# Routing in two parts, the new tokens second in the output projection, and a weight load in halves

## The chip, the cores and the metric

The kernel runs on one core of a Trainium2 chip, in one launch. The metric is the device time in microseconds (us); lower is better. Times of a stage are read from one profiled execution, in us from the start of its span.

## The reference, cut to what matters

One decoder layer: 512 prompt tokens and 64 new tokens (8 sequences of 8), width 1024, all in 32-bit floats. Two token mixers are merged into `m`; the tail, which the change touches, is:

```
x = x + g1 * (m @ w_o)                                  # w_o 1024 x 1024
h = rmsnorm(x, norm2) * (1 + sc2) + sh2
glog = h @ w_rg + b_rg ; elog = h @ w_re + b_re         # 4 groups, 32 experts
group = top-1 of glog ; experts = top-2 of elog inside the group
weight = softmax(two logits) * softmax(glog)[group]
for each expert e: out += weight_e * ((silu(h @ w_gate_e) * (h @ w_up_e)) @ w_down_e)   # 1024->256->1024
x = x + g2 * out ; y = rmsnorm(x, final_norm)
```

Each token goes to two of 32 experts. The weights of all experts are read from HBM: gate and up are 1 MB each, down is 1 MB, so 3 MB an expert.

## The kernel before, in words

The tail is one block of five instruction streams (sync SP, gpsimd POOL, scalar ACT, tensor PE, vector DVE) built from three stages, one behind the other on every engine: `merge_programs` (merge of the mixers, `w_o`, second norm, router logits), `expert_programs` (routing and experts) and `final_programs`. The order on each engine is written out by hand, and semaphores tie the engines together; an engine that waits holds everything behind it.

**`w_o` and logits.** The 576 tokens are five tiles (`NT = 5`; tile 4 has the 64 new tokens). `o_tile(t)` (L2140 to L2152) makes two 512-column products for a tile, and tile 4 makes both at once in two halves of the array (L2143). For each half DVE multiplies by the gate (L2277) and adds the residual (L2280); ACT squares (L2085), POOL makes the reciprocal root (L2044, L2046), DVE makes the normed rows (L2286, L2288). SP stores `x2` (L2013) and ACT stores `h2` (L2090) to scratch in HBM. PE transposes `h2` (L2161), ACT copies it out (L2094), PE makes 36 logits (L2172), DVE adds the bias (L2265). Tiles go 0, 1, 2, 3, 4. The per-sequence shift, scale and gate of the new tokens (`mod_new`) come by 16 DMAs from ACT's queue (L2076, L2077); DVE first waits for them when it reaches tile 4 (L2271).

**Routing.** When all five tiles' logits are there, DVE chooses group and experts for all tiles in one pass (L2567 to L2587), PE counts tokens per expert by bf16 products with 0/1 matrices, DVE works out for each of the 10 token-choice columns a block, a step and a slot (L2594 to L2630), PE multiplies one-hot matrices into a table of 25 steps (L2493), and DVE writes `pairs` and `toks` (L2640 to L2646). POOL waits for that table, then gathers rows of `h2` by indirect DMA (L2423).

**Experts.** Each of 17 fixed steps does two experts, 64 rows each. In a step PE does 8 transposes (L2502), 32 gate/up matmuls (L2514), 2 small transposes (L2521) and 16 down matmuls (L2531). Ahead of step 0 PE does 20 matmuls for the last block's rows (L2540). Gate/up weights (4 MB a step) have three buffers, down weights (2 MB a step) four. SP issues the loads (L2704, L2713) in this order: step 0, down 0, gate/up 1, the five `x2` stores, down 1 behind the last `w_o` product, down 2 behind the last `x2` store, gate/up 2 behind the `h2` stores, down 3 behind `overd` (the end of the routing's use of memory that down buffer 3 covers), then gate/up 3 behind `gmm >= 1`, that is the last gate/up matmul of step 0, and from there gate/up s+3 behind step s's gate/up product, down s+4 behind step s's down product.

The core of SP's loop, before:

```
sp.wait_ge(overd, 1)
load_down(sp, m, ins, 3, (6, 7))
...
if max(lo, GU_BUFS) <= g < hi:
    sp.wait_ge(gmm, s + 1)
    load_gate_up(sp, m, ins, g, experts(g))
```

Of the kernel before, what the change touches and what calls it, by code (L numbers as in the profile page):

```python
# [9 lines left out]
U32 = mybir.dt.uint32  # L10
# [1890 lines left out]
ROUTE_CONST = 64  # L1901
ROUND = 12582912.0
# [25 lines left out]
def expert_memory(nc, m):  # L1928
# [14 lines left out]
    m.iota, m.rc, m.rcb = tail("iota", [128, 128]), tail("route_const", [128, ROUTE_CONST]), tail("route_const_bf", [128, 280], BF16)  # L1943
    m.x2 = Region(nc, base + 99520)("x2", [128, NT, D])


def merge_programs(nc, m, ins, st, psum, sem):
# [16 lines left out]
    ss, rstd = sb(96256, "x2_ss", [128, NT]), sb(96288, "x2_rstd", [128, NT])  # L1964
# [34 lines left out]
    def sync(sp):  # L1999
# [11 lines left out]
        for t in range(NT):  # L2011
            sp.wait_ge(x2d, 2 * t + 2)
            sp.dma_start(m.x2_dram[tile_cols(t), :], m.x2[0:ROWS[t], t, :]).then_inc(x2st, 16)  # L2013
            if t == NT - 2:
                sp.wait_ge(omm, 10)
                load_down(sp, m, ins, 1, (2, 3))
        sp.wait_ge(h2d, NT)
        sp.wait_ge(x2st, 16 * NT)
        load_down(sp, m, ins, 2, (4, 5))
        sp.wait_ge(h2tr, NT)  # L2020
# [4 lines left out]
    def gpsimd(pool):  # L2025
# [14 lines left out]
        pool.dma_start(m.rbias[:, NG:36], ins["b_re"][0].partition_broadcast(128)).then_inc(rld, 16)  # L2040
        for t in range(NT):
# [3 lines left out]
            pool.wait_ge(rsd, 2 * t + 1)  # L2045
            p.tensor_tensor(q, q, m.half[:, 0:1], ALU.pow).then_inc(rsd, 1)  # L2046

    def scalar(act):
# [30 lines left out]
        act.wait_ge(init, 2)  # L2079

        def square(t):
            act.wait_ge(x2d, 2 * t + 2)
            if t:
                act.wait_ge(xsq, t)
            a.activation(junk[0:ROWS[t], :], m.x2[0:ROWS[t], t, :], ACT.Square, accum_out=ss[0:ROWS[t], t:t + 1]).then_inc(xsq, 1)  # L2085

        def keep_h2T(t):
            r = ROWS[t]
            act.wait_ge(h2d, t + 1)
            act.dma_start(m.h2_dram[tile_cols(t), :], h2[0:r, t % 2, :]).then_inc(h2st[t % 2], 16)  # L2090
            act.wait_ge(h2tr, t + 1)
            if t:
                act.wait_ge(lmm, t)
            a.copy(h2T[:, :, 0:r].rearrange("p (a c) t -> p a c t", a=2),  # L2094
                   psum[:, 4:6, :].rearrange("p a (c t) -> p a c t", t=128)[:, :, :, 0:r]).then_inc(h2ev, 1)
        square(0)
        for t in range(1, NT):
            keep_h2T(t - 1)
            square(t)
        keep_h2T(NT - 1)  # L2100

    def tensor(pe):
# [35 lines left out]
        def o_tile(t):  # L2138
            if t == 4:
                pe.wait_ge(oev, 6)  # L2140
                for c in range(KC):
                    for j in range(2):
                        last = te.matmul(psum[64 * j:64 * j + 64, j, :], mT[:, c, tile_cols(t)], wo[j][:, c, :],  # L2143
                                         start=c == 0, stop=c == KC - 1, tile_position=(0, 64 * j))
                last.then_inc(omm, 2)
                return
            for j in range(2):
                i = 2 * t + j
                if i >= 4:
                    pe.wait_ge(oev, i - 3)  # L2150
                for c in range(KC):
                    last = te.matmul(psum[0:ROWS[t], i % 4, :], mT[:, c, tile_cols(t)], wo[j][:, c, :], start=c == 0, stop=c == KC - 1)  # L2152
                last.then_inc(omm, 1)

        def h2_transposes(t):
            r = ROWS[t]
            pe.wait_ge(h2d, t + 1)
            if t:
                pe.wait_ge(h2ev, t)
            for c in range(KC):  # L2160
                last = te.transpose(psum[:, 4 + c // 4, 128 * (c % 4):128 * (c % 4) + r],  # L2161
                                    h2[0:r, t % 2, 128 * c:128 * c + 128], m.ident[0:r, 0:r])
            last.then_inc(h2tr, 1)

        def logits(t):
            r = ROWS[t]
            pe.wait_ge(h2ev, t + 1)
            pe.wait_ge(rld, 64)
            if t >= 2:
                pe.wait_ge(ld, t - 1)  # L2170
            for c in range(KC):
                last = te.matmul(psum[0:r, 6 + t % 2, 0:36], h2T[:, c, 0:r], wr[:, c, :], start=c == 0, stop=c == KC - 1)  # L2172
            last.then_inc(lmm, 1)

        o_tile(0)
        for t in range(1, NT):
            o_tile(t)
            h2_transposes(t - 1)
            logits(t - 1)
        h2_transposes(NT - 1)  # L2180
        logits(NT - 1)

    def vector(dve):
# [78 lines left out]
        def add_logits(t):  # L2262
            r = ROWS[t]
            dve.wait_ge(lmm, t + 1)
            v.tensor_tensor(m.logits[0:r, t, :], psum[0:r, 6 + t % 2, 0:36], m.rbias[0:r, :], ALU.add).then_inc(ld, 1)  # L2265

        for t in range(NT):
            r = ROWS[t]
            if t == NT - 1:
                dve.wait_ge(nld, 32 * NB)  # L2270
                v.scalar_tensor_tensor(modn[0:64, 2, :], modn[0:64, 2, :], 1.0, n2[0:64, :], ALU.add, ALU.mult).then_inc(sc2, 1)  # L2271
                dve.wait_ge(sc2, 2)
            for j in range(2):
                i = 2 * t + j
                dve.wait_ge(omm, i + 1)
                rows = slice(0, r) if t < 4 else slice(64 * j, 64 * j + 64)
                v.tensor_tensor(xs[0:r, j, :], psum[rows, i % 4, :], mod(t)[rows, 0, GW * j:GW * j + GW], ALU.mult).then_inc(oev, 1)  # L2277
                dve.wait_ge(oev, i + 1)
                x = m.x2[0:r, t, GW * j:GW * j + GW]
                v.tensor_tensor(x, x, xs[0:r, j, :], ALU.add).then_inc(x2d, 1)  # L2280
            dve.wait_ge(rsd, 2 * t + 2)
            if t >= 2:
                dve.wait_ge(h2tr, t - 1)
                dve.wait_ge(h2st[t % 2], 16 * (t // 2))
            h = h2[0:r, t % 2, :]
            v.scalar_tensor_tensor(h, m.x2[0:r, t, :], rstd[0:r, t:t + 1], mod(t)[0:r, 2, :], ALU.mult, ALU.mult).then_inc(hsc, 1)  # L2286
            dve.wait_ge(hsc, t + 1)
            v.tensor_tensor(h, h, mod(t)[0:r, 1, :], ALU.add).then_inc(h2d, 1)  # L2288
            if t:
                add_logits(t - 1)  # L2290
        add_logits(NT - 1)
# [4 lines left out]
def route_constants(nc, m, step):  # L2296
# [11 lines left out]
    step(p.iota(ints[:, 0:10], pattern=[[1, 2], [0, NT]], base=0, channel_multiplier=2))  # L2308
    step(p.tensor_copy(m.rcb[:, 256:266], ints[:, 0:10]))
    step(p.iota(ints[:, 0:10], pattern=[[0, 2], [1, NT]], base=1, channel_multiplier=0))  # L2310
# [3 lines left out]
def expert_programs(nc, m, ins, psum, sem):  # L2314
# [93 lines left out]
    def gpsimd(pool):  # L2408
# [24 lines left out]
        def run(lo, hi):  # L2433
# [8 lines left out]
            for s in range(lo, hi):  # L2442
                if s + 2 < hi:
                    gather(s + 2)
# [509 lines left out]
```

## Time and profile before

| | us |
|---|---|
| time, median of 3 runs (lowest, highest) | 1181.98 (1181.97, 1183.64) |
| the profiled execution's own time | 1181.74 |
| its span | 1180.0 |
| PE busy | 1069.7 (91%) |
| DVE busy | 560.2 (47%) |
| ACT busy | 250.2 (21%) |
| POOL busy | 154.4 (13%) |

The profiled execution spends 1.7 us outside its span. Busy shares are means over the whole layer; the change sits in the stretch from 784 us on, and the rows below are taken there. "PEclk" is TensorE's granted clock as a share of full speed. A DMA's "landing" is counted from its issue.

### The profile page before, as it was taken

The numbers are of one execution on the slowest core, as the hardware profiler recorded it, in microseconds if no ns is written. First come the engines' busy times: TensorE is split into PE (matmuls) and PEld (weight loads), VectorE is DVE, ScalarE is ACT, GpSimd is POOL, SyncE is SP. The second block draws the span as 40 slices with busy tenths as digits, with TensorE's granted clock in tenths as the row PEclk, the third lists the DMA queues.
The fourth block names the chain that finished last, engine by engine and source line by source line (L and its number), as shares of the span: only waits on it lengthen the run. The fifth ranks groups of instructions, "written<-read, shape, count | busy, mean of one in ns | idle before, by whom it ended". The sixth has DMA issues, their size and how long they took to land. (4 is left out here: it accounts for less than half of the span.)

```text
span 1180.0 us, 15016 instructions
## 1 busy us (share of the span) xinstructions
PE 1069.7 (91%) x5862; PEld 703.7 (60%) x5862; DVE 560.2 (47%) x1109; ACT 250.2 (21%) x673; POOL 154.4 (13%) x299
## 2 busy tenths in 40 slices
PE   5999998999999999899999999999946998978786
PEld 3455777777777887887577777754423333322222
DVE  3123737467788494475754455443264111110126
ACT  3100010567622222464111010101110110100011
POOL 3000500012314000041100000100011211111101
PEclk8999998999999999899999999999967999998998
DMA  9995543252414443124462422359176999999975
GB/s 334 340 258 181 192 77 75 43 128 69 74 50 72 107 80 73 37 73 144 125 223 83 111 75 89 123 138 327 77 286 222 416 420 415 418 419 418 412 290 175
DMA packets 96852, 226.32 MB, mean 192 GB/s; under 512 B 21422, under 2 KB 40167, under 8 KB 84082
## 3 DMA queue, kind: packets, MB, share of 16 engines
q1 hardware_dynamic: 86998, 202.70, 52.5%
q10 hardware_dynamic: 4660, 12.75, 3.1%
q0 software_dynamic: 5120, 9.88, 2.3%
q8 instruction: 48, 0.79, 0.3%
q14 instruction: 26, 0.21, 0.1%
HBM read 210.60 MB, written 23.08 MB: 198 GB/s over the span
## 5 line engine op out<-in xcount | busy, mean ns | idle before, releaser
L2514 PE MATMUL ps<-w_gate_up,xT 128*64 128x512 f32 x528 | 129.5, 630 | 20.5 <-DMA w_gate_up<-w_e_up 20.5
L2514 PEld LDWEIGHTS ps<-w_gate_up,xT 128*64 128x64 f32 x528 | 41.2, 145 | 105.9 <-issue 76.8
L2676 DVE TENSOR_TENSOR act<-silu_gate,ps 128x256 f32<-128x256 f32 x17 | 7.1, 420 | 199.1 <-ACT silu_gate L2469 199.1
L695 PE MATMUL ps<-hT,w_ring 128*128 128x288 f32 x384 | 97.5, 414 | 3.7 <-PEq L105 3.7
L695 PEld LDWEIGHTS ps<-hT,w_ring 128*128 128x128 f32 x384 | 73.9, 195 | 23.9 <-issue 4.0
L2531 PE MATMUL ps<-w_down,actT 128*64 128x512 f32 x264 | 62.1, 599 | 8.8 <-DVE actT L2680 8.8
L1345 PE MATMUL ps<-hT,w_ring 128*128 128x288 f32 x264 | 67.8, 407 | 0.0
L1630 DVE SCALAR_TENSOR_TENSOR conv_y<-z_staged,convT,conv_y 128x600 f32<-128x600 f32 x72 | 59.7, 842 | 9.3 <-ACT conv_y L1080 7.5
L1345 PEld LDWEIGHTS ps<-hT,w_ring 128*128 128x128 f32 x264 | 49.4, 190 | 13.1 <-issue 0.5
L2531 PEld LDWEIGHTS ps<-w_down,actT 128*64 128x64 f32 x264 | 18.0, 136 | 41.2 <-issue 29.1
L2429 POOL DMA_INDIRECT pair_scratch<-y_block,pairs x16 | 16.0, 1003 | 200.7 <-ACT y_block L2477 200.7
L2469 ACT ACTIVATE silu_gate<-ps 128x256 f32<-128x256 f32 x17 | 6.5, 383 | 129.7 <-PE ps L2514 129.7
L2477 ACT COPY y_block<-ps 128x1024 f32<-128x1024 f32 x16 | 16.2, 1012 | 83.7 <-PE ps L2531 83.7
L2152 PE MATMUL ps<-w_ring,mT 128*128 128x512 f32 x64 | 31.8, 654 | 2.3 <-issue 2.3
L2113 PE MATMUL ps<-T_mixers,w_ring 128*128 128x288 f32 x128 | 33.7, 406 | 0.0
L1080 ACT ACTIVATE conv_y<-z_staged,convT 128x600 f32<-128x600 f32 x24 | 19.1, 796 | 67.7 <-DVE z_staged L1710 58.9
L1411 PE MATMUL ps<-hT,w_ring 128*128 128x288 f32 x128 | 32.8, 411 | 0.0
L423 PE MATMUL ps<-w_ring,hT 128*128 128x512 f32 x64 | 31.1, 643 | 1.2 <-DVE hT L572 1.2
L2210 DVE TENSOR_TENSOR pair_sums<-pair_sums,ps 128x288 f32<-128x288 f32 x14 | 6.4, 454 | 50.7 <-PE ps L2113 50.7
L1411 PEld LDWEIGHTS ps<-hT,w_ring 128*128 128x128 f32 x128 | 23.8, 190 | 10.5 <-issue 3.0
L454 PE MATMUL ps<-w_ring,hT 128*128 128x512 f32 x64 | 29.7, 625 | 0.0
L2502 PEld LDWEIGHTS ps<-ident,x_gathered 128*128 128x128 f32 x136 | 17.1, 196 | 19.3 <-issue 13.0
(539 smaller groups left out, 1995.2 us busy)
## 6 DMA issues: line engine op xcount, KB each, us to landing
w_down<-w_e_down SPq DMA_DIRECT2D x32, 1024.0 KB, 23.6
w_ring<-w_in SPq DMA_DIRECT2D x15, 2048.0 KB, 13.8
w_gate_up<-w_e_gate SPq DMA_DIRECT2D x30, 1024.0 KB
w_gate_up<-w_e_up SPq DMA_DIRECT2D x30, 1024.0 KB
w_ada_slots<-w_ada SPq DMA_DIRECT2D x8, 2048.0 KB, 8.4
w_ada_slots<-w_ada SPq DMA_DIRECT2D x4, 1024.0 KB, 15.0
w_ring<-w_pa SPq DMA_DIRECT2D x2, 2048.0 KB, 7.9
w_ring<-w_pb SPq DMA_DIRECT2D x2, 2048.0 KB, 7.9
```

The costliest lines, as they stand in the source:

```text
L423: last = te.matmul(psum[:, zv_bank(t), :], m.hT[:, c, tile_cols(t)], zv0[:, c, :], start=c == 0, stop=c == KC - 1)
L454: last = te.matmul(psum[:, zv_bank(i), :], m.hT[:, c, tile_cols(t)], zv1[:, c, :], start=c == 0, stop=c == KC - 1)
L695: last = nc.tensor.matmul(psum[:, bank + hf, 0:HALF], w[:, c, 128 * q:128 * q + 128], x[:, c, HALF * hf:HALF * hf + HALF], start=c == 0, s ...
L1080: a.activation(y[:, n % 2, 0:TAPPED], stage(n)[:, 0:TAPPED], ACT.Copy, scale=m.convT[:, CH[n]:CH[n] + 1]).then_inc(tap, 1)
L1345: last = te.matmul(psum[:, k % 4, 0:HALF], w[:, c, :], x(c), start=c == 0, stop=c == 3)
L1411: last = te.matmul(psum[:, b, 0:HALF], w0[:, c, 128 * n:128 * n + 128], hT[:, c, HALF * hf:HALF * hf + HALF], start=c == 0, stop=c == KC - 1)
L1630: v.scalar_tensor_tensor(out, stage(n)[:, j:j + TAPPED], wt, out, ALU.mult, ALU.add).then_inc(cstep if j < HIST else conv, 1)
L2113: last = te.matmul(psum[:, n % 8, 0:HALF], w[:, c, :], x[:, c, :], start=c == 0, stop=c == 3)
L2152: last = te.matmul(psum[0:ROWS[t], i % 4, :], mT[:, c, tile_cols(t)], wo[j][:, c, :], start=c == 0, stop=c == KC - 1)
L2502: last = te.transpose(psum[:, 2 + c // 4, 128 * (c % 4):128 * (c % 4) + 128], xg[:, s % 2, c::KC], m.ident[:, :])
L2514: last = te.matmul(psum[side(u), s % 2, :], xT[:, s % 2, c, side(u)], gu[s % GU_BUFS][:, u, :, c, :], start=c == 0, stop=c == KC - 1)
L2531: last = te.matmul(psum[side(u), 4 + hf, :], aT[:, s % 2, c, side(u)], wd[s % WD_BUFS][:, u, c, 512 * hf:512 * hf + 512], start=c == 0, st ...
```

## The change

**`merge_programs`.** The tiles are taken in the order `ORDER = (0, 4, 1, 2, 3)`; a position p stands for the place in that order. PE's order is:

```
+        o_half(0, 0, whole)
+        o_half(0, 1, whole)
+        o_new(1)
+        h2_transposes(0)
+        o_half(2, 0, range(0, 2))
+        logits(0)
+        o_half(2, 0, range(2, KC))
+        for p in range(2, NT):
+            if p > 2:
+                o_half(p, 0, whole)
+            h2_transposes(p - 1)
+            if p == 3:
+                constant_logits()
+            o_half(p, 1, range(0, 4))
+            logits(p - 1)
+            o_half(p, 1, range(4, KC))
+        early_counts()
+        last_transposes(0)
+        logits(END, range(0, 4))
+        table(0, EARLY_POS)
+        last_transposes(1)
+        logits(END, range(4, KC))
+        late_counts()
+        table(EARLY_POS, NT)
```

The last tile's rows are transposed and multiplied with the router before their norm: `scaled(j)` is x2 times the scale, and the reciprocal root and the part of the logits that comes of the shift (`constant_logits`) are put in when the logits are read. DVE's order from the second tile on:

```
+        second_norm(0)
+        dve.wait_ge(nld, 32 * NB)
+        v.scalar_tensor_tensor(modn[0:64, 2, :], modn[0:64, 2, :], 1.0, n2[0:64, :], ALU.add, ALU.mult).then_inc(sc2, 1)
+        dve.wait_ge(sc2, 2)
+        residual(1, 0)
+        residual(1, 1)
...
+        choose_experts(nc, dve, m, r, 0, EARLY_POS, 0)
+        second_norm(3)
+        choose_experts(nc, dve, m, r, 0, EARLY_POS, 1)
+        residual(END, 0)
+        scaled(0)
+        split_pairs(nc, dve, m, r, 0, EARLY_POS)
+        add_logits(3)
+        slot_rows_of(nc, dve, m, r, 0, EARLY_POS, psum[:, 2, 0:96])
+        residual(END, 1)
+        scaled(1)
+        dve.wait_ge(rsd, 2 * END + 4)
+        dve.wait_ge(x4tr, 2)
+        v.scalar_tensor_tensor(h, h, rstd[:, END:], modp[:, 1, :], ALU.mult, ALU.add).then_inc(h2d, 1)
+        v.scalar_tensor_tensor(m.logits[:, END, :], psum[:, 6 + END % 2, 0:36], rstd[:, END:], r.const[:, :], ALU.mult, ALU.add).then_inc(ld, 1)
+        choose_experts(nc, dve, m, r, EARLY_POS, NT, 0)
+        choose_experts(nc, dve, m, r, EARLY_POS, NT, 1)
+        split_pairs(nc, dve, m, r, EARLY_POS, NT)
+        slot_rows_of(nc, dve, m, r, EARLY_POS, NT, psum[:, 3, 0:64])
+        ... 3 small operations, then the table: pairs and toks of the 16 regular steps
```

`choose_experts` is the choice of L2570 to L2587 for the positions lo to hi (12 operations in part 0, 6 in part 1, one more at its end). `split_pairs` makes the step one-hots by 6 small operations. `slot_rows_of` waits for PE's counts, then does 2 products, 2 sums and 2 * (hi - lo) comparisons against the slot numbers. The slot of a choice comes straight from the count, and the old chain over blocks and overflow steps (12 small operations with their own one-hots) is put off:

```
+        def run(lo, hi):
+            if lo == 0:
+                over_blocks()
+                weights()
             x_evacuate(lo)
+            if lo == 0:
+                over_counts()
+                over_pairs()
             for s in range(lo, hi):
+                if s == 1:
+                    over_slots()
                 dve.wait_ge(sgd, s + 1)
+                if s == 1:
+                    over_table_columns()
...
                 if s + 1 < hi:
                     x_evacuate(s + 1)
```

`over_slots()` is 12 small operations, 3 on 90 elements and 10 comparisons on 128 elements, and ends in

```
+            last.then_inc(over_hot, 1)
+            dve.wait_ge(over_hot, 1)
+            v.nop().then_inc(constd, 1)
```

PE makes the table of the overflow steps by 20 small matmuls behind step 1's gate/up product.

**SP.** Down 2 waits for the last `x2` store as before, gate/up 2 for the `h2` stores. Then:

```
-        sp.wait_ge(overd, 1)
-        load_down(sp, m, ins, 3, (6, 7))
+        load_down_of(sp, m, ins, 3, 0, 6)
+        sp.wait_ge(constd, 1)
+        load_down_of(sp, m, ins, 3, 1, 7)
...
-                if max(lo, GU_BUFS) <= g < hi:
+                if g == GU_BUFS:
+                    sp.wait_ge(first_half_used, 1)
+                    load_gate_up_half(sp, m, ins, g, experts(g), 0)
+                    sp.wait_ge(gmm, s + 1)
+                    load_gate_up_half(sp, m, ins, g, experts(g), 1)
+                elif max(lo, GU_BUFS) <= g < hi:
                     sp.wait_ge(gmm, s + 1)
                     load_gate_up(sp, m, ins, g, experts(g))
```

`load_down_of` loads one expert's 1 MB; `load_gate_up_half` loads 4 times 512 KB. `first_half_used` is raised behind the 16th of step 0's 32 gate/up matmuls. The upper half of down buffer 3 lies over the constants that routing and `over_slots` read.

**POOL.** The waits of the routing go, but for those on the `h2` stores and the table; the clearing of the gathered rows goes, and that of `y_last` (L2416) moves behind the first two gathers. `final_programs` reads the weights by position; nothing else of it changes.

## Rows read from the trace of the kernel before

**Rows 1.** Stretches: PE, PEld, DVE, ACT, POOL busy; PEclk, DMA share, GB/s.
```profile
836.00:838.00 2.00, 2.00 (x4) 0.85 (x3) 1.52 (x3) 0.00 (x0) 0.00 (x0) 0.50 0.00 0
875.00:887.00 12.00, 0.83 (x7) 0.61 (x7) 10.92 (x44) 0.32 (x2) 0.89 (x1) 0.50 1.01 426
887.00:893.00 6.00, 0.93 (x10) 0.64 (x10) 5.56 (x26) 0.00 (x0) 1.23 (x2) 0.50 0.08 34
904.00:910.00 6.00, 5.96 (x32) 2.57 (x28) 0.42 (x2) 0.38 (x1) 0.00 (x0) 1.00 0.22 40
911.00:1117.00 206.00, 178.52 (x804) 67.58 (x800) 28.22 (x43) 20.55 (x29) 29.25 (x29) 0.96 1.02 418
```
**Rows 2.** Timeline of SP's issues from 835 us: start, us, what.
```profile
864.42 0.47 SPq L2013 DMA_DIRECT2D x_scratch<-x  x1
870.65 1.04 SPq L2713 DMA_DIRECT2D w_down<-w_e_down  x2
...
892.64 0.81 SPq L2713 DMA_DIRECT2D w_down<-w_e_down  x2
908.56 0.33 SPq L2704 DMA_DIRECT2D w_gate_up<-w_e_gate  x1
```
**Rows 3.** The chain that ended last, from 891 us: start, us, what.
```profile
891.00 0.19 DVE toks L2646
891.47 4.58 DMA x_gathered<-h_scratch,toks
...
901.50 7.02 PE ps L2514 x32
```
**Rows 4.** Timeline of PE, from 780 us.
```profile
792.48 7.03 PE L2152 MATMUL ps<-w_o_second,mT 128*128 128x512 f32 x16
834.78 8.81 PE L2152 MATMUL ps<-w_ring,mT 128*128 128x512 f32 x16
...
852.43 1.97 PE L2172 MATMUL ps<-w_router,h2T 128*128 128x36 f32 x16 [1.10 <-ACT h2T L2094]
854.34 0.64 PE L2143 MATMUL ps<-w_ring,mT 128*64 128x512 f32 x1
...
861.36 1.09 PE L2161 MATMUL ps<-ident,h 128*128 128x128 f32 x8
```
**Rows 5.** ACT's DMA queue from 781.6 to 810 us: packets, MB, share of 16 engines.
```profile
q10 hardware_dynamic: 256, 1.05, 14.2%
```
**Rows 6.** Timeline of DVE, from 835 us.
```profile
850.50 0.69 DVE L2277 TENSOR_TENSOR x_step<-ps,mod_prompt 128x512 f32<-128x512 f32 x1 [5.45 <-PE ps L2152]
855.69 1.23 DVE L2288 TENSOR_TENSOR h<-h,mod_prompt 128x1024 f32<-128x1024 f32 x1
856.93 1.21 DVE L2271 SCALAR_TENSOR_TENSOR mod_new<-mod_new,norm2b 64x1024 f32<-64x1024 f32 x1
874.12 0.89 DVE L2578 TENSOR_SCALAR pen<-gone 128x20 f32<-128x20 f32 x1
875.75 0.33 DVE L2567 TENSOR_TENSOR one<-em,mv 128x160 f32<-128x160 f32 x1
885.54 0.17 DVE L2624 SCALAR_TENSOR_TENSOR slot<-side__5605,s 128x10 f32<-128x10 f32 x1
886.86 2.04 DVE L2630 TENSOR_SCALAR onehot_slot<-iota,slot 128x128 bf16<-128x128 f32 x10
910.34 1.21 DVE L2668 COPY xT<-ps 128x1024 f32<-128x1024 f32 x1
```
**Rows 7.** POOL's clearing beside the choice, from its timeline.
```profile
873.17 1.80 POOL L2415 MEMSET x_gathered<- 128x2048 f32 x1 [6.70 <-DVE logits L2265]
```
**Rows 8.** Gathers, issue to landing: the one of 891.47, of 892.95, all 17.
```profile
x_gathered<-h_scratch,toks POOLq DMA_INDIRECT x1, 4.6
x_gathered<-h_scratch,toks POOLq DMA_INDIRECT x1, 9.5
x_gathered<-h_scratch,toks POOLq DMA_INDIRECT x17, 10.3
```

More of the change, by code:

```diff
@@ L1901 @@
 ROUTE_CONST = 64
+ORDER = (0, 4, 1, 2, 3)
+POS = {t: p for p, t in enumerate(ORDER)}
+PROWS = [ROWS[t] for t in ORDER]
+EARLY_POS = 3
+EMPTY = 2304.0
+SIDE = 1024.0
 ROUND = 12582912.0
@@ new lines, in split_pairs @@
+def split_pairs(nc, dve, m, r, lo, hi):
+    v = nc.vector
+    at, shape = slice(lo, hi), [128, 2, hi - lo, NE // 2]
+    one = r.one[:, :, at, :].rearrange("p k t (s u) -> p k t s u", u=2)
+    for k in range(2):
+        last = v.tensor_tensor(r.onehot_step[:, k, at, :], one[:, k, :, :, 0], one[:, k, :, :, 1], ALU.add)
+    last.then_inc(r.split, 1)
+    dve.wait_ge(r.split, 1 if lo == 0 else 2)
+    for x, part in enumerate((r.high, r.low)):
+        for k in range(2):
+            last = v.tensor_tensor(r.parts[:, x, k, at, :], r.onehot_step[:, k, at, :],
+                                   part[:, k, at].unsqueeze(2).broadcast_to([128, hi - lo, NE // 2]), ALU.mult)
@@ new lines, in slot_rows_of, with step @@
+def slot_rows_of(nc, dve, m, r, lo, hi, counts):
+    v = nc.vector
+    at, n = slice(lo, hi), hi - lo
+    def step(i):
+        r.n += 1
+        i.then_inc(r.step, 1)
+        dve.wait_ge(r.step, r.n)
+    dve.wait_ge(r.counted, 1 if lo == 0 else 2)
+    for k in range(2):
+        i = v.tensor_tensor(r.prod[:, k, at, :], r.one[:, k, at, :], counts.rearrange("p (t e) -> p t e", e=NE), ALU.mult)
+        if k:
+            step(i)
+    for k in range(2):
+        i = v.tensor_reduce(r.v[:, k, at], r.prod[:, k, at, :], AX.X, ALU.add)
+        if k:
+            step(i)
+    for k in range(2):
+        for p in range(lo, hi):
+            last = v.tensor_scalar(r.onehot_slot[:, k, p, :], m.slots[:, :], r.v[:, k, p:p + 1], None, ALU.is_equal)
+    last.then_inc(r.hot, 1)
@@ L2096, in scalar, with square @@
-        square(0)
[L2097 to L2100, printed above, removed]
+        act.wait_ge(init, 3)
+        act.wait_ge(mld, 32)
+        act.wait_ge(win, 7 * PAIRS)
+        a.copy(h2[64:65, 1, :], modp[64:65, 1, :]).then_inc(shd, 1)
+        def square(p):
+            rows = PROWS[p]
+            act.wait_ge(x2d, 2 * p + 2)
+            if p:
+                act.wait_ge(xsq, p)
+            a.activation(junk[0:rows, :], m.x2[0:rows, ORDER[p], :], ACT.Square, accum_out=ss[0:rows, p:p + 1]).then_inc(xsq, 1)
@@ L2175, in tensor, with o_half @@
[L2175 to L2181, printed above, removed]
+        def o_half(p, j, cs):
+            tile, i = ORDER[p], 2 * p + j
+            if i >= 4 and cs[0] == 0:
+                pe.wait_ge(oev, i - 3)
+            for c in cs:
+                last = te.matmul(psum[:, i % 4, :], mT[:, c, tile_cols(tile)], wo[j][:, c, :], start=c == 0, stop=c == KC - 1)
+            if cs[-1] == KC - 1:
+                last.then_inc(omm, 1)
@@ new lines, in late_counts, with table @@
+        def late_counts():
+            pe.wait_ge(r.chosen, 2)
+            te.matmul(psum[:, 3, 0:32], r.strict, both[:, 3, :], start=False, stop=False)
+            te.matmul(cut(psum[:, 3, 32:96]), r.onesb, two(both[:, 3, :]), start=False, stop=False)
+            te.matmul(psum[:, 3, 32:64], r.strict, both[:, 4, :], start=False, stop=False)
+            te.matmul(psum[:, 3, 64:96], r.onesb, both[:, 4, :], start=False, stop=True).then_inc(r.counted, 1)
+        def table(lo, hi):
+            pe.wait_ge(r.hot, 1 if lo == 0 else 2)
+            for p in range(lo, hi):
+                rows = PROWS[p]
+                for k in range(2):
+                    for x in range(2):
+                        last = te.matmul(psum[:, 2, 128:144], r.onehot_slot[0:rows, k, p, :], r.parts[0:rows, x, k, p, :],
+                                         start=p == k == x == 0, stop=p == END and k == x == 1)
+            if hi == NT:
+                last.then_inc(r.tabled, 1)
@@ L2260, in vector @@
         dve.wait_ge(init, 2)
[L2262 to L2290, printed above, removed]
```

550 lines of the change are left out of this document (345 added, 205 removed).

## The prediction

> **What bounds the kernel now.** The view by stretches comes first, since the page's busy shares average over stages with other limits. From 911 to 1117 us the DMA engines are full (share 1.02, 418 GB/s) while PE works 178.5 of 206 us [rows 1]. 418 GB/s times 206 us is 86 MB: the weights from gate/up 3 on, and the gathers and scatters beside them. The expert stage is therefore a train of bytes of fixed length, and its end moves with its start. Just before it, from 904 to 910, the DMA engines do nearly nothing (40 GB/s) [rows 1]. What starts the train is the next question, and SP's issues answer it: gate/up 3 is issued at 908.56 [rows 2], 0.04 us after the first gate/up product ends at 901.50 + 7.02 = 908.52 [rows 3]. The chain back from there: table written at 891.20, gather landed at 896.05, transposes and 20 extra matmuls to 901.50 [rows 3]. So the quantity to follow is the instant at which gate/up 3 gets the DMA engines. The weights ahead of it are hidden whatever their order, if they have landed by then: from 887 to 893 the queues ran dry too (34 GB/s) [rows 1].
>
> **A, the `w_o` stage: to the end of its last product.** Before, it ends at 861.36, where tile 3's transposes start [rows 4]. A half tile of `w_o` is 6.86 us (the row reads 7.03, of which 0.17 lies over the next one's start), tile 4's double product 861.36 - 854.34 = 7.02, eight transposes 1.09, a tile's logits 854.34 - 852.43 = 1.9, and each time PE idled 1.10 for ACT's copy [rows 4]. The new order fills those three 1.1 us holes with `w_o` columns (-3.3), but now has all four sets of transposes and logits ahead of the last product, instead of three (+2.9), and the constant product (+0.2).
> Then two stalls. First, the new tokens come second, and their scale and gate come by 16 DMAs that now are needed early. By 810 us ACT's queue had moved 1.05 MB, just what those 16 DMAs write (8 x 96 KB + 8 x 32 KB) [rows 5]; I take them as landed at 810. DVE is ready for them at 805.7 (tile 0's second half ends at 792.48 + 6.86 = 799.34, and the norm comes 6.4 later: from 850.50, 0.2 after such an end, to 855.69 + 1.23 = 856.92 with gate, add, square, root and two norm operations, less 0.2 for a logits addition between [rows 4, 6]). Then 1.21 for the scale [rows 6], four half operations of 0.73, 2.1 for square and root, 2.5 for the norm: transposes of the new tokens from about 818.8, while PE has nothing left from 816.1. Stall 2.7. Second, the norm of position 3 stands behind 12 operations of the early choice; it is ready about 0.3 us after PE. Last, the clock: in the stretch behind 834.78 a half tile took 8.81 instead of 6.86 with a granted clock of 0.50, that is 1.2 of 2.4 GHz [rows 1, 4], after PE had paused for ACT's copy and worked on small tiles. It is inside the 861.36. I keep it, since the new order has a pause too.
> 861.36 - 3.3 + 2.9 + 0.2 + 2.7 + 0.3 = 864.1. Term A: +2.7. Ends: -1.9 (transfers by 806, no dip), +4.5 (transfers at 812).
>
> **B, from the last product to the table.** Before: 861.36 to 891.20, 29.8 us. After, from T = the last product's end: counts 0.7; DVE's early slots (2 products and 2 sums of some 0.25 each, 6 comparisons of 0.2 [rows 6]) to T+2.8; residual and scale to T+5.0; square, four small POOL operations to T+6.4; one 1.28 us operation on 1024 columns and the logits to T+7.9. Late choice: 12 + 7 dependent operations at about 0.2 on 20 elements and 0.26 on 64 (0.17 and 0.33 are the rows for 10 and 160, and a gap of 0.03 follows [rows 6]) = 4.6, to T+12.5. `pen` took 0.89 before on 20 elements [rows 6], and it ended at 875.01 with POOL's clearing, 873.17 + 1.80 = 874.97 [rows 7]; that clearing is gone, so I take 0.2. Six small operations 0.9, late slots 1.6, three small operations 0.3, the last 8 table products 0.7, two table operations 0.4: T+16.3. Term B: 16.3 - 29.8 = -13.5. What went: the pass over all five tiles becomes one over two, and the 12-step chain over blocks goes behind the first gather. Ends: -15 to -11 (cold PE, `pen` at 0.9). The table then stands at 864.1 + 16.3 = 880.4.
>
> **C, the gather.** Before, issued at 891.47 and landed 4.58 later [rows 3]: nothing was on the queues (34 GB/s from 887 to 893 [rows 1]), and down 3 was issued only at 892.64 [rows 2]. After, issued at about 880.7, where down 2 and gate/up 2 are in flight. The last `x2` store, now 512 KB, goes at about T+4.3 and lands near 875 (before: issue 864.42, down 2 behind its landing at 870.65 [rows 2]); down 2 follows, `h2`'s last store at T+7.9 lets gate/up 2 go by 877, and with down 3's first MB behind that the DMA engines have 7.3 MB, some 17 us at 426 GB/s [rows 1], to about 893. A gather among loads takes 9.5 (the one of 892.95) or 10.3 (median of 17, nearly all in the full stretch) [rows 8]. I take 10.0 as against 4.6. Term C: +5.4. Ends: 0 and +6.7.
> The Trainium skill (DMA: Bandwidth & Descriptors, section Queues, rings and completion order) says that each DMA engine takes turns between its queues, a packet at a time. By that alone the gather would lose only its turn, the first rival below, and the sum would come to +0.3; the trace's gathers among loads do not agree (9.5, 10.3).
> Gathered: about 890.9. DVE's four small operations over counts and the 10 weight columns (about 5.5 us) end before that and cost nothing. If the gather came at 885 they would come to the edge of the path.
>
> **D, from the gather to step 0's last gate/up matmul.** Transposes, 20 matmuls, 32 matmuls: 908.52 - 896.05 = 12.5 [rows 3], unchanged. It ends at 903.4. Term D: 0.
>
> **E, from there to gate/up 3.** Before 0.04. After, the text of SP decides. SP takes its instructions in order, and ahead of both halves of gate/up 3 stands the wait for `constd` and the second MB of down 3. `constd` is raised at the end of `over_slots`, and DVE runs that under `s == 1`: behind step 0's activation and behind `x_evacuate(1)`. Before, DVE left that copy at 910.34 + 1.21 = 911.55 [rows 6], 3.0 us after 908.52. Then 12 dependent operations at 0.17 with gaps, 2.5; three on 90 elements, 0.6; 10 comparisons 2.0 [rows 6]; the last wait 0.1: 5.2. So `constd` comes 8.2 us after the product whose middle was to release the first half: both halves' own waits have long been met, and the halving wins nothing. Queued behind that wait on SP: down 3's second half, gate/up 3, down 4 and all the rest; for 13 us or so, from 893 to after 911, the DMA engines stand idle again.
> Behind `constd` comes 1.05 MB of down 3, which used to be landed by then: 1.05 / 0.418 = 2.5 us [rows 1]. In return step 0's scatter and the fourth gather fall partly into the idle time: about half of 1 MB, 1.0 us. Term E: 8.2 + 0.1 + 2.5 - 1.0 = +9.8. Ends: +8.3 and +11.5.
> Halves of 512 KB with 4 KB rows: no row prices this alone; zero, at most 0.3.
>
> **Sum.** A +2.7, B -13.5, C +5.4, D 0, E +9.8: +4.4. On the profiled execution's 1181.74 that is 1186.1; the median of the runs shown, 1181.98, is 0.2 above it. I forecast 1186.0. Behind the train nothing is changed: last step and final stage keep their length.
>
> **Rivals.**
> Gather hardly slowed (18%). Its 128 rows are 0.52 MB, 1.25 us at 418 GB/s; at half that rate it takes 1.25 us more than the 4.6 alone, 5.9. For it: it has a queue of its own, and the loads fill only SP's. Against: both rows of gathers among loads. At 4.6 to 5.9 us: 1180.7 to 1182.0, no slower than before. It decides from a gather below about 8 us (then the sum is under +2.4).
> The train is not what counts (8%): PE's steps set the end, and starting step 0 earlier pays at once: -5.1 (908.5 to 903.4), 1176.6. It needs PE to be the later one at step 3 and on. For it: PE's share is high. Against: 178.5 of 206 us busy beside a DMA share of 1.02 [rows 1]. This one ends faster than before; it decides if the idle DMA time up to 911 can be caught up by less than 11 us of slack.
> More is late than I count (12%): `over_slots` slowed by PE's and POOL's traffic, or the late choice on a cold PE, or the new tokens' transfers at 812: +3, 1189.
> My forecast (62%), by itself 1182.5 to 1189.
> That the change doesn't do what it says is part of the forecast: the halves are not loaded while the first product runs.
>
> **Range and chances.** The ends of the terms and the rivals give 1178.5 to 1190.5 for 8 in 10. 0.2% is 2.4 us, about what a measurement of this kernel tells from none. Faster than 1179.6: nearly all of the second rival, a third of the first: 14%. Within: most of the rest of the first and a quarter of the forecast's case: 27%. Slower: 59%.
>
> **What would show it.** SP waits for DVE's `constd` and issues down 3's second half about 8 us after step 0's last gate/up matmul; DMA share near 0 for over 10 us before; table some 11 us earlier than 891.2; first gather 9 to 10 us; PE idle 2 to 3 us ahead of the new tokens' transposes. Wrong, if gate/up 3 is issued before step 0's product ends, or if the first gather lands in 5 us, or if PE does not wait for weights from step 4 on.

## The result and the profile after

Timed beside each other, eight runs of each kernel: before 1182.1 us (1178.1 to 1184.9), after 1188.9 us (1185.7 to 1192.2). The ratio is 1.0059, with a 95% interval of 1.0043 to 1.0074: slower by 7.0 us (6.8 between the medians). The forecast was 1186.0, slower by 4.4. The profiled executions have spans of 1180.0 and 1187.0, so they carry the same 7.0.

First SP, from its timeline of the changed kernel (start, us, what it issued):

```profile
874.49 0.96 SPq L2987 DMA_DIRECT2D w_down<-w_e_down  x2
...
877.41 0.65 SPq L2973 DMA_DIRECT2D w_gate_up<-w_e_up  x1
878.10 32.83 SPq L2978 DMA_DIRECT2D w_down<-w_e_down  x2
910.97 0.80 SPq L2954 DMA_DIRECT2D w_gate_up<-w_e_gate  x1
```

The last row but one holds two DMAs, the two halves of down 3. The first goes at 878.10; the second is issued at 910.60 and ends the group at 910.93. Between them SP waits, by its waits (engine and line, what it waited for: us in total, times, longest):

```profile
SPq L2978 <- DVEq L2903: 32.1, 1, 32.1
```

L2903 raises `constd`. DVE's timeline shows how late that is: the copy for step 1, then the small operations of `over_slots` (the first of them is the second row), then its ten comparisons.

```profile
904.25 1.21 DVE L2915 COPY xT<-ps 128x1024 f32<-128x1024 f32 x1
905.38 0.16 DVE L2883 TENSOR_SCALAR q<-r__5606 128x10 f32<-128x10 f32 x1
...
908.46 2.06 DVE L2900 TENSOR_SCALAR onehot_over_slot<-iota,slot 128x128 bf16<-128x128 f32 x10
```

The chain that ended last, of the changed kernel (start, us, what), answers to [rows 3]:

```profile
880.87 9.27 DMA x_gathered<-h_scratch,toks
...
892.15 3.18 PE ps L2805 x20
895.33 7.02 PE ps L2777 x32
...
1092.79 30.85 DMA w_gate_up<-w_e_up
1123.68 9.83 PE ps L2777 x32
```

The same end of the chain in the kernel before:

```profile
1087.31 29.87 DMA w_gate_up<-w_e_up
1117.23 9.46 PE ps L2514 x32
```

Step 0's gate/up matmuls end at 895.33 + 7.02 = 902.35, 6.2 us earlier than before. Gate/up 3 follows at 910.97, 2.4 us later than before. The last load that PE waits for, gate/up of the last step but one, lands at 1092.79 + 30.85 = 1123.64, before at 1117.18; below, this is called the last weights' landing, and the train is the time from the first weights issued (in the changed kernel down 3's second half) to it. What lies between is seen in the stretches (PE, PEld, DVE, ACT, POOL busy; PEclk, DMA share, GB/s):

```profile
900.00:910.00 10.00, 9.48 (x48) 3.79 (x46) 6.07 (x26) 1.40 (x2) 0.62 (x1) 1.00 0.00 1
912.00:917.00 5.00, 5.00 (x44) 2.72 (x40) 0.66 (x3) 0.38 (x1) 0.00 (x0) 1.00 0.92 347
917.00:922.00 5.00, 4.48 (x22) 1.51 (x23) 1.56 (x2) 0.57 (x1) 0.00 (x0) 1.00 0.94 305
950.00:1000.00 50.00, 40.67 (x180) 14.67 (x178) 5.93 (x9) 4.19 (x6) 5.71 (x7) 0.93 1.02 418
```

Ten microseconds of nothing, then ten at 347 and 305 GB/s, and only then the 418 of [rows 1]. The `w_o` stage, from the timeline of PE (in brackets the idle time before and what ended it), answers to [rows 4]:

```profile
820.61 0.72 PE L2314 MATMUL ps<-ident,h 65*128 65x65 f32 x8 [3.94 <-DVE h L2505]
821.16 5.35 PE L2295 MATMUL ps<-w_o_second,mT 128*128 128x512 f32 x8
...
838.95 3.70 PE L2295 MATMUL ps<-w_o_second,mT 128*128 128x512 f32 x8
864.38 0.21 PE L2348 MATMUL ps<-route_const_bf 128*128 128x96 bf16 x1
```

PE idles 3.94 us ahead of the new tokens' transposes, and the eight matmuls behind that take 5.35 us instead of 3.70. The granted clock of that stretch is 0.51, the lower of the two levels (1.2 of 2.4 GHz):

```profile
822.00:824.00 2.00, 2.00 (x4) 0.86 (x3) 0.00 (x0) 0.00 (x0) 0.00 (x0) 0.51 1.02 420
```

The whole difference, stretch by stretch (before's numbers from [rows 2 to 4], but for the landing at 1117.18 and for the first row, which is the start of its `w_o` stage):

```profile
783.84 8.80 PE L2152 MATMUL ps<-w_ring,mT 128*128 128x512 f32 x16 [2.25 <-issue]
```

| stretch | before | after | difference | forecast |
|---|---|---|---|---|
| stages ahead, to the first `w_o` matmul | 783.84 | 784.31 | +0.5 | 0 |
| A: to the end of `w_o` | 77.52 | 80.07 | +2.6 | +2.7 |
| B: to the table | 29.8 | 16.2 | -13.6 | -13.5 |
| C: table to gather landed | 4.85 | 9.57 | +4.7 | +5.4 |
| D: gather to step 0's last gate/up matmul | 12.5 | 12.2 | -0.3 | 0 |
| E1: to the next weights issued | 0.04 | 8.25 | +8.2 | +8.3 |
| E2: from there to the last weights landed | 208.6 | 213.0 | +4.4 | +1.5 |
| behind that | 62.8 | 63.4 | +0.5 | 0 |

The table is written at 880.41 + 0.17 (the last row of that step on DVE):

```profile
880.41 0.17 DVE L2563 TENSOR_SCALAR toks<-pairs 128x16 uint32<-128x16 uint32 x1
```

### The profile page after: what moved, and what is told of

It reads as the page before. It is cut to its first block, busy times and chain, and to the rows that moved or that the text cites. A ratio compares the mean times of both kernels' runs of the same rounds, so it can differ in the third digit from the quotient of the medians.

```text
span 1187.0 us, 15168 instructions
## 1 busy us (share of the span) xinstructions
PE 1073.6 (90%) x5901; PEld 702.2 (59%) x5901; DVE 567.6 (48%) x1158; ACT 252.0 (21%) x677; POOL 154.7 (13%) x307
## 4 chain that ended last, share of the span: by engine, by line
PE 27%; SPq 11%; DMA 8%; DVE 3%; issue 1%; ACTq 0%; ACT 0%; POOL 0%; DVEq 0%
PE ps L2265 16%; SPq L2973 8%; DMA w_gate_up<-w_e_up 5%; PE ps L2777 4%; SPq L2987 3%; PE ps L2295 2%; DMA mod_new<-mod_scratch 2%; PE ps L2796 1%; PE ps L3080 1%; DMA x_gathered<-h_scratch,toks 1%; PE ps L2332 1%; PE ps L3070 0%; PE ps L3083 0%; PE ps L2765 0%; PE ps L2805 0%
## 5 line engine op out<-in xcount | busy, mean ns | idle before, releaser
L2777 PE MATMUL ps<-w_gate_up,xT 128*64 128x512 f32 x528 | 132.5, 645 | 28.3 <-DMA w_gate_up<-w_e_up 28.3
L2755 ACT COPY y_block<-ps 128x1024 f32<-128x1024 f32 x16 | 16.2, 1012 | 84.6 <-PE ps L2796 84.6
L423 PE MATMUL ps<-w_ring,hT 128*128 128x512 f32 x64 | 31.1, 643 | 1.2 <-DVE hT L572 1.2
L2295 PE MATMUL ps<-w_o_second,mT 128*128 128x512 f32 x64 | 30.7, 628 | 0.0
L2765 PEld LDWEIGHTS ps<-ident,x_gathered 128*128 128x128 f32 x136 | 17.1, 196 | 22.3 <-issue 12.2
```

The lines of the kernel that those rows point to most:

```text
L423: last = te.matmul(psum[:, zv_bank(t), :], m.hT[:, c, tile_cols(t)], zv0[:, c, :], start=c == 0, stop=c == KC - 1)
L2295: last = te.matmul(psum[:, i % 4, :], mT[:, c, tile_cols(tile)], wo[j][:, c, :], start=c == 0, stop=c == KC - 1)
L2777: last = te.matmul(psum[side(u), s % 2, :], xT[:, s % 2, c, side(u)], gu[s % GU_BUFS][:, u, :, c, :], start=c == 0, stop=c == KC - 1)
```

## The experiments

The stages ahead of `w_o` differ by up to 6.6 us between executions of kernels that are equal there (the first `w_o` matmul is at 779.2 in E10 and at 785.9 in E1). Traces are therefore compared over "w_o to end" (first `w_o` matmul to the end of the span: 396.2 before, 402.7 after) and "w_o to landed" (the same start to the last weights' landing: 333.3 and 339.3). The timed medians of the kernel before in the four groups of runs were 1182.1, 1181.6, 1181.8 and 1183.9. The ratios are those on record, with their 95% intervals; they are not quite the quotients of the medians, and where the two differ in a comparison of runs from different groups, both are given.

| run | timed | ratio to before | w_o to end | w_o to landed |
|---|---|---|---|---|
| e1_gu3_ahead_of_constd | 1177.0 | 0.9965 [0.9950, 0.9980] | 390.7 | 328.2 |
| e2_gu3_whole | 1177.6 | 0.9977 [0.9960, 0.9994] | 390.5 | 328.0 |
| e3_slots_early | 1180.8 | 0.9990 [0.9973, 1.0007] | 394.0 | 332.4 |
| e4_before_halves | 1179.2 | 0.9970 [0.9952, 0.9987] | 393.4 | 331.2 |
| e5_gather_first | 1182.5 | 1.0012 [0.9998, 1.0027] | 397.4 | 335.7 |
| e6_gate_up1_after_mod | 1189.7 | 1.0065 [1.0042, 1.0087] | 404.4 | 341.6 |
| e7_both_sp_changes | 1177.3 | 0.9945 [0.9925, 0.9966] | 393.6 | 329.6 |
| e8_both_and_mod | 1175.0 | 0.9936 [0.9914, 0.9959] | 392.4 | 329.2 |
| e9_mod_first | 1172.4 | 0.9920 [0.9899, 0.9940] | 386.1 | 322.9 |
| e10_both_gather_first | 1176.2 | 0.9954 [0.9939, 0.9969] | 390.9 | 328.5 |
| e11_changed_mod_first | 1182.6 | 1.0012 [0.9995, 1.0028] | 397.6 | 334.7 |
| e12_all_four | 1167.4 | 0.9856 [0.9839, 0.9873] | 383.5 | 321.7 |

### E1: gate/up 3 ahead of the wait for the constants

The changed kernel, with one wait and one load of SP put further back:

```
-        sp.wait_ge(constd, 1)
-        load_down_of(sp, m, ins, 3, 1, 7)
...
                     sp.wait_ge(gmm, s + 1)
                     load_gate_up_half(sp, m, ins, g, experts(g), 1)
+                    sp.wait_ge(constd, 1)
+                    load_down_of(sp, m, ins, 3, 1, 7)
```

> The changed kernel with SP's wait for constd and down 3's second half moved behind both halves of gate/up 3; nothing else. Theory (the weight train's start sets the end, and the wait for constd holds it): first half issued at about 899, second at 902.4, down 3's second half at 910.7; the DMA engines run from 901 on instead of 913, some 10 to 12 us less, about 1178. Rival (PE's steps set the end): no change, 1188. Rival (gate/up loads in halves are themselves slow and cost the gain): above 1183.

SP's timeline in this run:

```profile
900.90 0.33 SPq L2954 DMA_DIRECT2D w_gate_up<-w_e_gate  x1
...
904.33 0.33 SPq L2954 DMA_DIRECT2D w_gate_up<-w_e_gate  x1
...
912.53 0.33 SPq L2978 DMA_DIRECT2D w_down<-w_e_down  x1
```

The first half goes out in the middle of step 0's product and the second at its end. Timed -11.9 us against the changed kernel (1188.9 to 1177.0; 11.1 by the two ratios), in the traces -12.0. That is more than the 8.25 us of the wait, since the first half now also starts in the middle of the product. The wait on SP is the largest single cost of the change, and without it the new kernel is faster than the old one.

### E2: gate/up 3 whole, behind the first product

E1 with the load in one piece, so that only the place of the wait for `constd` differs from the kernel before:

```
-                    sp.wait_ge(first_half_used, 1)
-                    load_gate_up_half(sp, m, ins, g, experts(g), 0)
                     sp.wait_ge(gmm, s + 1)
-                    load_gate_up_half(sp, m, ins, g, experts(g), 1)
+                    load_gate_up(sp, m, ins, g, experts(g))
                     sp.wait_ge(constd, 1)
                     load_down_of(sp, m, ins, 3, 1, 7)
```

> As the run before, but gate/up 3 is one load of four 1 MB transfers behind step 0's last gate/up matmul. Theory: issued at 902.4, train from 904.4, some 8.5 us earlier than in the changed kernel: 1179 to 1180. If the halves' smaller rows cost 2 us of rate (350 GB/s and less in the first 10 us of the changed kernel's train), this one comes within 1 to 2 us of the one with halves although it starts 3.5 us later; if they cost nothing, it is 3.5 us slower than that one.

Its issue on SP, and the stretch behind it (columns as above):

```profile
901.41 0.33 SPq L2971 DMA_DIRECT2D w_gate_up<-w_e_gate  x1
```
```profile
903.50:913.50 10.00, 10.00 (x48) 3.26 (x48) 5.58 (x26) 1.01 (x1) 2.04 (x2) 1.00 0.98 400
```

400 GB/s where the halves had 347 and 305. The landing comes at 1112.53, so the train is 1112.53 - 901.41 = 211.1 us, and 208.6 without the added MB (2.5): that of the kernel before. Timed, E1 and E2 can't be told apart (0.9965 and 0.9977, intervals overlapping). By the traces the halves start the train earlier and use that up again: E1's is 213.1 from 900.90. The expectation, 1179 to 1180, was missed by 1.4 us on the fast side: it counted the earlier start alone, and the train is 1.9 us shorter as well (213.0 to 211.1).

### E3: `over_slots` early

The changed kernel, SP as changed; only DVE's order differs:

```
                 over_counts()
                 over_pairs()
+                over_slots()
             for s in range(lo, hi):
-                if s == 1:
-                    over_slots()
```

> The changed kernel with over_slots moved ahead of step 0's activation, behind over_pairs, where DVE idles 5 us; SP's order as in the changed kernel. Theory: constd at about 903.1 instead of 910.6, the whole train 7.5 us earlier, 1181 to 1182; step 0's activation waits at most 0.5 us. Rival (PE's steps set the end): no gain, or 0.5 us slower.

SP's timeline, and the activation of step 0 on DVE:

```profile
903.48 0.33 SPq L2977 DMA_DIRECT2D w_down<-w_e_down  x1
903.85 0.43 SPq L2953 DMA_DIRECT2D w_gate_up<-w_e_gate  x1
```
```profile
904.29 0.42 DVE L2932 TENSOR_TENSOR act<-silu_gate,ps 128x256 f32<-128x256 f32 x1 [0.90 <-ACT silu_gate L2747]
```

The activation isn't held up, and the train starts at 903.48 instead of 910.60. Timed -8.1 us. It is the same wait, shortened instead of moved, so both repairs confirm one cause. E1's is the better: 3.3 us shorter in the traces, and it needs nothing from DVE. The landing is at 1115.93, a train of 212.45, or 210.0 without the added MB: 1.4 more than before, at 342 GB/s in its first ten microseconds:

```profile
905.00:915.00 10.00, 9.48 (x46) 3.32 (x47) 1.56 (x2) 1.01 (x1) 2.03 (x2) 1.00 0.96 342
```

### E4: the kernel before, with the halves only

```
-                if max(lo, GU_BUFS) <= g < hi:
+                if g == GU_BUFS:
+                    sp.wait_ge(first_half_used, 1)
+                    load_gate_up_half(sp, m, ins, g, experts(g), 0)
+                    sp.wait_ge(gmm, s + 1)
+                    load_gate_up_half(sp, m, ins, g, experts(g), 1)
+                elif max(lo, GU_BUFS) <= g < hi:
```

> The kernel before with the halves alone: gate/up 3 in halves, the first behind the 16th of step 0's gate/up matmuls; routing, order of tiles and down 3 as before. Theory: the train starts 3.5 us earlier (905.0 instead of 908.56), less up to 2 us that small rows may cost: 1178.5 to 1180.5. Rival (halves are slow): no gain, 1182 or more.

Its first issue:

```profile
902.36 0.33 SPq L2705 DMA_DIRECT2D w_gate_up<-w_e_gate  x1
```

Timed 3 us faster than before, ratio 0.9970. Landed at 1112.09, a train of 209.7: 1.1 longer than in one piece. So the halving is worth something on the old kernel, where nothing stands ahead of it on SP, and nothing on the new one, where both of its own waits are over when SP comes to them.

Where the time goes is seen in two stretches of this run:

```profile
904.00:909.00 5.00, 4.48 (x26) 2.07 (x24) 1.98 (x3) 0.38 (x1) 0.00 (x0) 1.00 0.89 287
909.00:914.00 5.00, 5.00 (x26) 1.72 (x24) 0.00 (x0) 1.01 (x1) 1.01 (x1) 1.00 1.03 420
```

Only SP's queue moves bytes in both, in packets that are all under 8 KB (386 with 1.43 MB, then 577 with 2.10). The first five microseconds run at 287 GB/s, the next five at full rate. E1 (270 from 903 to 908, then 417) and E9 (292 from 895 to 900, then 419) show the same. So neither the smaller packets by themselves nor a meeting with the gather or scatter is what costs; why the first half is slow stays open.

### E5: the first gather ahead of the loads

The changed kernel; gate/up 2 and the first MB of down 3 wait for the first gather's landing:

```
-        load_gate_up(sp, m, ins, 2, (4, 5))
...
+        sp.wait_ge(gth[0], 16)
+        load_gate_up(sp, m, ins, 2, (4, 5))
         load_down_of(sp, m, ins, 3, 0, 6)
```

> The changed kernel with gate/up 2 and down 3's first MB issued only when the first gather has landed (a wait on SP, nothing else). Theory (the loads in flight slow the first gather from 4.6 to 9.3 us): first gather lands in under 5 us, step 0's last gate/up matmul, constd and the train 4.4 us earlier; gate/up 2 and down 3's first half then still land before constd: about 4.4 us less than the changed kernel, 1184.5. Rival (DVE's 10 comparisons beside it hold up the gather's descriptors): the gather still takes over 8 us and nothing is gained. Rival (the later loads push the train): slower than 1189.

The gather in the chain of this run:

```profile
877.40 4.32 DMA x_gathered<-h_scratch,toks
```

4.32 instead of 9.27 us. DVE's 10 comparisons start 2.4 us behind the gather's issue in both kernels (at 879.83 here, at 883.30 in the changed kernel), and POOL's issues are the same: the loads on SP's queue are what slows it. Timed 6.4 us less than the changed kernel (5.6 by the two ratios, each beside its own runs of before), in the traces 5.3.

### E6: gate/up 1 behind the transfers for the new tokens

The changed kernel, to see whether gate/up 1 delays the 16 transfers for which the new tokens' scale waits:

```
+        sp.wait_ge(nld, 32 * NB)
         load_gate_up(sp, m, ins, 1, (2, 3))
```

> The changed kernel with gate/up 1's load held on SP until the 16 transfers of the new tokens' shift, scale and gate have landed. Theory (PE stands 3.9 us before the new tokens' transposes, because these transfers land at 811 behind 10 MB of weights): with 6 MB in front they land some us earlier, and up to 3.9 us of the stall go; 1185 to 1187. Rival (the 16 transfers take 28 us by themselves, whatever else is in flight): no change, 1189.

SP's wait, and PE's stall:

```profile
SPq L2974 <- DMA mod_new<-mod_scratch: 26.7, 1, 26.7
```
```profile
817.23 1.13 PE L2315 MATMUL ps<-ident,h 65*128 65x65 f32 x8 [4.01 <-DVE h L2506]
```

The stall is 4.01 instead of 3.94, and the time is that of the changed kernel. This theory fell: in the 26.7 us in which SP waited, gate/up 0 and down 0, issued before it, were in flight all the same. From 782 to 807 all queues together moved only 222 GB/s although the DMA engines were full:

```profile
782.00:807.00 25.00, 25.00 (x84) 10.73 (x82) 5.28 (x6) 3.20 (x4) 0.76 (x2) 0.95 1.03 222
```

### E7: E1 and E3 together

Both diffs as above.

> The changed kernel with gate/up 3's halves ahead of the wait for constd, and over_slots moved ahead of step 0's activation as well. Theory: over the run with SP's order alone (1177.0) little is left, since its DMA engines had no gap between gate/up 3 and down 3's second half; 1175.5 to 1177.5. If it is 3 us or more faster, that gap was real.

1177.3, ratio 0.9945; against E1's 0.9965 the intervals overlap. Once gate/up 3 stands ahead of the wait, no gain from raising `constd` earlier can be told. A new short gap shows in the stretch before and behind the first issue: share 0.41.

```profile
898.00:904.00 6.00, 6.00 (x30) 1.77 (x26) 5.22 (x27) 1.10 (x1) 0.00 (x0) 1.00 0.41 102
```

### E8: E7 with gate/up 1 held, E9: with all of SP's weights held

E8 adds the wait of E6 to E7. E9 puts the same wait ahead of gate/up 0, so that none of the experts' weights move until the 16 transfers have landed:

```
+        sp.wait_ge(nld, 32 * NB)
         load_gate_up(sp, m, ins, 0, (0, 1))
```

> The run before with gate/up 1 held until the 16 transfers have landed. If that hold takes away the stall on PE, everything behind it moves up by as much, 3 to 4 us: 1172.5 to 1174. If the stall stays, as the run before.

> The run with both SP changes, and on SP all loads of expert weights (gate/up 0, down 0, gate/up 1) held until the 16 transfers of the new tokens' shift, scale and gate have landed. Theory (they take 27 us only because they share the DMA engines with gate/up 0 and down 0): they land before 799, PE's stall of 3.9 us goes, and all behind it moves up: 1172.5 to 1174.5 against 1177.3. The held loads still end by 830, long before step 0. Rival (the 16 transfers are slow by themselves): still near 810, no change.

E8 kept the stall (DVE idled 6.26 us for `mod_new`), and its ratio, 0.9936, can't be told from E7's. E9 has 0.9920, and its PE timeline shows no stall ahead of the new tokens:

```profile
814.40 0.66 PE L2315 MATMUL ps<-ident,h 65*128 65x65 f32 x8
```

In the traces w_o to end is 386.1, 7.5 less than E7's, and w_o to landed 6.7 less. Timed it is 4.9 less, 3.0 by the ratios, and their intervals overlap: E7's profiled execution was 1.7 us above its median, E9's 2.4 below. That the hold pays is shown by E11, where the intervals don't overlap; here the missing stall speaks for it.

### E10: E7 with the gather first

E7 and E5's edit, to see what an earlier gather is worth when SP no longer waits for the constants.

> The run with both SP changes, and gate/up 2 and down 3's first MB held until the first gather has landed. The gather should again land in under 5 us and step 0 end 4.4 us earlier. But now nothing stands between the DMA engines and the train except bytes: the 5 MB held back fill the stretch that stood idle (3 to 5 us of it in the run without the hold). Theory (with constd out of the way, bytes set the end): no gain of 4.4, between 1175.5 and 1179. Rival (step 0's time still sets the start): 1173.

The gather took 4.38 us. The weights landed only 1.0 us earlier than in E7. Timed, the two can't be told apart: by the medians E10 is 1.1 us faster, by the ratios (0.9954 and 0.9945) as much slower. Nearly all of the 5 us is lost again: the loads that were held for the gather must still pass.

### E11: the changed kernel with only the hold of E9

> The changed kernel with only the hold of all expert weights until the 16 transfers have landed. If the stall in w_o goes, table, constd and train come 3.9 us earlier: 1185. If it stays: 1189.

PE's timeline at the new tokens' transposes, then the stretch with the 16 transfers alone:

```profile
812.17 0.66 PE L2315 MATMUL ps<-ident,h 65*128 65x65 f32 x8
812.67 3.65 PE L2296 MATMUL ps<-w_o_second,mT 128*128 128x512 f32 x8
```
```profile
784.00:794.00 10.00, 10.00 (x25) 4.45 (x24) 1.38 (x2) 0.47 (x1) 0.00 (x0) 1.00 0.41 56
```

The `w_o` stage takes 74.2 us instead of 80.1. The 5.8 are the stall (3.94), the eight matmuls behind it (5.35 to 3.65, 1.7), and 0.2 left over. Timed -6.3 us (5.6 by the ratios). Without that stall the new order of the stage is 3.3 us shorter than before's 77.5. The forecast of this run, made from the stall alone, was too small, since it left out the clock behind it.

### E12: all four

E9 and E5's edit together: gate/up 3 ahead of the wait, `over_slots` early, weights behind the 16 transfers, gather ahead of gate/up 2.

> All four edits: gate/up 3 ahead of constd, over_slots early, expert weights held until the new tokens' transfers have landed, gate/up 2 and down 3's first MB held until the first gather has landed. Theory (bytes set the end, and the hold behind the gather only moves them): within 1.5 us of the run without the last hold (1172.4), so 1171 to 1174. If the gather's 4.4 us were still worth their length: 1168.

1167.4 against 1183.9 of the kernel before in the same group: ratio 0.9856, 16 to 17 us faster than before, and the best version that was run. Gate/up 3 is issued at 888.00. The gather in its chain, and the stretch that was the hole in E9 (there 134 GB/s from 888 to 895):

```profile
874.80 4.36 DMA x_gathered<-h_scratch,toks
```
```profile
885.00:890.00 5.00, 5.00 (x26) 1.65 (x24) 4.38 (x21) 1.39 (x2) 0.00 (x0) 1.00 1.02 424
```

Just ahead of gate/up 3 no idle DMA time is left. The expectation, 1171 to 1174, was missed on the good side, and the time is the one named for the case that the gather's 4.4 us are worth their length (1168). The traces don't bear that case out: from the first `w_o` matmul the weights land 1.2 us earlier than in E9 (321.7 and 322.9), and the part behind is 1.5 shorter. Timed, it is 5.0 us less than E9, 7.6 by the ratios, so 2.3 to 4.9 us stay open. E9's profiled execution lay 2.4 us below its median and this one 1.3 above; the two ran in different groups, and single executions of one kernel spread by 3 to 9 us.

## Why the prediction was right, and where it was too small

**The mechanism was right.** Faster routing was won and then lost on SP: table at 880.6 (forecast 880.4), down 3's second half 8.25 us behind step 0's last gate/up matmul (forecast 8.3), DMA share 0 for ten microseconds ahead of it. E1 and E3 take that wait away in two ways and get 11.9 and 8.1 us back. On the idle time the prediction doesn't agree with itself: it says 13 us and also "from 893 to after 911", which is 18. The loads ahead of the wait ran until about 899, not 893, and the engines stood idle for 12 us. Reading SP's queue in its order, and adding up what DVE does ahead of `constd`, gave all but the size.

**The term that was mis-sized is E's last part, the length of the train.** The prediction had +2.5 for the added MB, -1.0 for scatter and gather in the idle time, and "zero, at most 0.3" for the halves: +1.5. Measured +4.4, 2.9 more, which is more than the whole miss of 2.6 (7.0 instead of 4.4). The credit of 1.0 was nearly right: the gathers' and scatters' queue moved 6.88 MB in the train instead of 7.18, 0.7 us. The MB is right by E2, whose train is 2.5 longer than before's. That leaves the halves. Taken from 2.4 us behind the first issue in both kernels, the next ten ran at 342 GB/s, against 404 before:

```profile
913.00:923.00 10.00, 9.48 (x66) 4.30 (x64) 2.22 (x5) 1.40 (x2) 0.28 (x1) 1.00 0.96 342
```
```profile
911.00:921.00 10.00, 10.00 (x49) 3.20 (x45) 0.55 (x1) 1.01 (x1) 2.02 (x2) 1.00 1.00 404
```

So 0.62 MB are missing, 1.5 us at 418 GB/s. The trains say the same. With the added MB, nine traces with halves (the changed kernel, E1, E3, E5 to E9, E11) have trains of 212.5 to 213.1, and E2, in one piece, 211.1; without it E4 has 209.7 against 208.6. The halves cost 1.1 to 2.0 us. E4's stretches rule out the meeting with the scatter, and the packet size as the only cause; which of the rest it is stays open, and some 1.1 us of this term (4.4 - 2.5 - 1.5 + 0.7) have no place in the traces.

The prediction says that no row prices the halves alone. The trace of the kernel before had one. It loads its last step in halves too, and from 1123 to 1127 all packets of SP's queue are under 8 KB, as in E4:

```profile
1123.00:1127.00 4.00, 4.00 (x21) 1.37 (x18) 0.00 (x0) 0.27 (x1) 0.00 (x0) 1.00 0.95 347
```

By that row 4.2 MB take about 2 us more than at 418 GB/s, near the 1.1 to 2.0 measured, where the prediction took nothing.

**A: the sum was right, with two errors in it.** The stall was 3.94 instead of 2.7, since the 16 transfers came at 811.8, not 810. DVE's row shows it:

```profile
811.79 1.22 DVE L2519 SCALAR_TENSOR_TENSOR mod_new<-mod_new,norm2b 64x1024 f32<-64x1024 f32 x1 [5.67 <-DMA mod_new<-mod_scratch]
```

The early choice ahead of the last product cost nothing instead of 0.3, and the rest of the stage was about 1 us shorter than counted. The low clock was kept in the sum, rightly: it moved from 836 to 822, behind the new stall. E11 shows that stall and clock belong together. With no pause ahead of them the eight matmuls run at full clock.

**B** came out at 16.2 for 16.3. `pen` took 0.17 us in the early choice, on 12 elements, and 0.18 in the late one, with POOL's clearing gone (850.25 and 873.90 on DVE); the 0.2 taken for it held.

**C** was 9.27, below the forecast 10.0 and close to the row of 9.5 among loads. The first rival, a gather hardly slowed by the loads, is refuted: 9.1 to 9.4 in the changed kernel and the eight runs with loads in flight, against 4.32, 4.38 and 4.36 in E5, E10 and E12 without. The Trainium skill (DMA: Bandwidth & Descriptors, section Queues, rings and completion order) has the engines take turns between queues. By turns alone the gather would have taken some 5.9 us by the estimate in the prediction, and no gather here among loads agrees. That rule gives no bound for a gather's latency in this kernel.

**The second rival**, that PE's steps and not the train set the end, is refuted too. Step 0's product ended 6.2 us earlier and the end came 7 later, and in E10 a gather 5 us faster moved the end by 1. E5 gained its gather's 5 us only because there PE's product, DVE's `constd` and so the held train all hang on the gather. That is read from the code and the traces; E10, the same hold with gate/up 3 free of `constd`, gained only 1.0 in the traces, as it should.

**The tail** grew by 0.5: the last gate/up product took 9.83 instead of 9.46, and no term stood for that.

## What to carry to other kernels

In a kernel that ends in a long train of loads, follow the instant at which the first held load of the train gets out, in the order of the issuing engine. An early wait for a small thing (here a buffer freed by some late small operations) holds everything behind it, so put loads whose own conditions come first ahead of it. Work that is moved earlier also moves its small transfers among the large ones. A latency from an idle stretch (4.3 us) is then the wrong row, and a small transfer that others wait for is best issued while nothing else is in flight. Halving a load gains what it starts earlier, less what the halves lose in rate (here 1 to 2 us of 3.4), and it gains nothing if a wait ahead of it on the same queue ends later.

## What the runs showed of the hardware that was not expected

- The 16 transfers of 1.05 MB in all that spread single rows over partitions moved 56 GB/s alone, at a DMA share of 0.41. In E11 they were issued from 777.7 to 782.9 and had landed at 794.1, when SP's hold ended: 16 us from the first issue. Beside the weights it was 30 us (782.1 to 811.8 in the changed kernel), and all queues together moved only 222 GB/s at a full share (E6's stretch). Holding the weights for 12 us cost nothing that shows, and took the stall away.
- A gather of 128 rows took 4.3 to 4.7 us alone and 9.1 to 9.4 among loads that keep SP's queue full.
- A load in halves, behind idle DMA engines, ran at 270 to 292 GB/s for five microseconds and then, in packets of the same size, at 417 to 420 (E1, E4, E9); the same bytes in one piece ran at 400 to 404 over ten.
- A pause of 3.94 us on PE was followed by a granted clock of 0.51 for several matmuls, and cost 1.7 us on top of itself. In E1, after a pause of 3.50 us, the same transposes and eight matmuls took 2.7 us more than in E11.
